# A two-layer hybrid flow trunk on one core: the edges of the expert stage, the squares of the norms and the last norm rearranged

## What is computed

```python
for l in range(DEPTH):                                  # DEPTH = 2
    sh1, sc1, gt1, sh2, sc2, gt2 = ada_mod(cond, w_ada[l], b_ada[l])   # silu(cond) @ w_ada + b_ada
    h = rms_norm(y, g_attn[l]) * (1 + sc1) + sh1
    ... # three head groups: neighbourhood attention, latent attention, windowed attention
    y = y + gt1 * (concat(o_na, o_mla, o_swa) @ w_out[l])
    h = rms_norm(y, g_ffn[l]) * (1 + sc2) + sh2
    y = y + gt2 * moe(h)        # 16 experts in 4 groups; best group, then the top 2 of it
y = rms_norm(y, g_final)
```

## Time and profile before

| what | value |
|---|---|
| median of 3 runs | 1250.95 us (1248.72 to 1256.21) |
| the profiled execution | 1255.41 us |
| its span in the profile | 1253.4 us |
| TensorE busy | 1152.9 us, 92% |
| VectorE busy | 772.4 us, 62% |
| ScalarE busy | 632.9 us, 50% |
| mean granted clock of TensorE | 0.947 of full |
| moved by the DMA queues | 314.35 MB |

### The profile page before, as it was taken

The page is one execution under the profiler, slowest core; times in us unless marked ns, Lnnn a source line. Parts: engine busy times, 40 slices in busy tenths (PEclk is TensorE's granted clock), DMA queues, the critical chain, the costliest instruction groups (busy, mean ns, idle before and its releaser), DMA issues.

```text
span 1253.4 us, 14864 instructions
## 1 busy us (share of the span) xinstructions
PE 1152.9 (92%) x5574; PEld 844.6 (67%) x5574; DVE 772.4 (62%) x1056; ACT 632.9 (50%) x751; POOL 127.8 (10%) x157
## 2 busy tenths in 40 slices
PE   6999998897899999999879998889789999999956
PEld 5576354554788888888666754455578888888846
DVE  1312356427698888888451233742768888988845
ACT  2201455315377777777320035631447777777721
POOL 2241100310100101010010011000000101010000
PEclk9899999999799999999969998999779999999985
DMA  9994478339489999999699140002549999999621
GB/s 330 335 309 169 145 264 280 100 109 377 148 321 372 359 376 366 383 375 367 221 345 240 68 168 16 1 1 81 245 158 352 369 375 378 377 364 369 257 87 75
DMA packets 81257, 314.35 MB, mean 251 GB/s; under 512 B 22766, under 2 KB 27100, under 8 KB 68396
## 3 DMA queue, kind: packets, MB, share of 16 engines
q1 hardware_dynamic: 65548, 279.17, 61.2%
q0 software_dynamic: 13152, 24.96, 6.0%
q10 hardware_dynamic: 2496, 9.44, 2.0%
HBM read 308.11 MB, written 26.38 MB: 267 GB/s over the span
## 4 chain that ended last, share of the span: by engine, by line
PE 84%; DVE 7%; issue 3%; ACT 3%; DMA 2%; SPq 0%; ACTq 0%; POOL 0%; POOLq 0%; DVEq 0%
PE bank L813 17%; PE bank L1072 14%; PE bank L1066 14%; PE bank L1067 14%; PE bank L795 3%; PE bank L941 3%; PE bank L820 3%; PE bank L740 2%; PE bank L1056 2%; PE bank L955 2%; ACT work L1295 2%; PE bank L733 2%; PE bank L973 1%; PE bank L1046 1%; PE bank L874 1%
## 5 line engine op out<-in xcount | busy, mean ns | idle before, releaser
L1791 DVE TENSOR_TENSOR ring_r<-ring,work_r 128x4096 fp32r<-128x4096 f32 x96 | 421.6, 4416 | 0.1
L1352 ACT ACTIVATE work_r<-ring 128x4096 fp32r<-128x4096 f32 x96 | 349.6, 3644 | 138.0 <-PE bank L1067 104.4
L1066 PE MATMUL bank<-work_r 128*128 128x512 f32 x768 | 310.1, 404 | 12.3 <-issue 5.1
L1067 PE MATMUL bank<-work_r 128*128 128x512 f32 x768 | 303.9, 396 | 0.0
L813 PE MATMUL bank<-hT,ring 128*128 128x384 f32 (+1 forms) x640 | 213.7, 493 | 3.3 <-ACT hT L1202 1.9
L1072 PE MATMUL bank<-ring_r,work_r 128*128 128x512 f32 x768 | 195.1, 396 | 0.4 <-DVE ring_r L1791 0.4
L813 PEld LDWEIGHTS bank<-hT,ring 128*128 128x128 f32 (+1 forms) x640 | 121.5, 192 | 88.0 <-issue 11.6
L1066 PEld LDWEIGHTS bank<-work_r 128*128 128x128 f32 x768 | 147.5, 192 | 43.9 <-issue 5.8
L1072 PEld LDWEIGHTS bank<-ring_r,work_r 128*128 128x128 f32 x768 | 144.2, 188 | 34.5 <-DVE ring_r L1791 0.8
L1067 PEld LDWEIGHTS bank<-work_r 128*128 128x128 f32 x768 | 147.1, 192 | 29.6
L1174 ACT ACTIVATE work<-bank 128x384 f32<-128x384 f32 (+6 forms) x79 | 38.0, 494 | 179.7 <-PE bank L813 89.3
(11 more groups left out here) (202 smaller groups left out, 1152.7 us busy)
## 6 DMA issues: line engine op xcount, KB each, us to landing
ring<-in_w_gate SPq DMA_DIRECT2D x32, 2048.0 KB, 11.5
ring<-in_w_up SPq DMA_DIRECT2D x32, 2048.0 KB, 12.3
ring<-in_w_down SPq DMA_DIRECT2D x32, 2048.0 KB, 12.3
ring<-in_w_ada SPq DMA_DIRECT2D x24, 2048.0 KB, 10.0
ring<-in_w_in SPq DMA_DIRECT2D x4, 2048.0 KB, 15.5
work<-yscr ACTq DMA_DIRECT2D x6, 1024.0 KB, 7.1
ring<-in_w_out SPq DMA_DIRECT2D x4, 1280.0 KB, 8.0
ring<-in_w_in SPq DMA_DIRECT2D x12, 256.0 KB, 6.9
```

The costliest lines, as they stand in the source:

```text
L1066: mm(b[:], x_hi[:, k, :], hi[:, k, half, :], start=(k == 0), stop=False)
L1067: last = mm(b[:], x_lo[:, k, :], hi[:, k, half, :], start=False, stop=False)
L1352: A_(w_hi[:, slot % 2, :], ring[slot][:], ACT.Copy).then_inc(s_hi, 1)
L1791: tt(ring_r[slot][:], ring[slot][:], w_hi[:, slot % 2, :].bitcast(F32), ALU.subtract).then_inc(s_lo, 1)
```

## The change

1. *Start.* g_final is no longer turned with the small vectors, the constant `rot` goes, and three more constants are cast to bf16.
2. *Squares.* VectorE adds the four blocks of each half tile in one reduction (`add_piece`, fp32, reading with a step of 384 words) into `sqr`; TensorE sums one product for each half tile instead of four. This holds at the start and behind layer 0.
3. *Expert 0's gate weights* are split by ScalarE and VectorE behind op5 of the output projection (`EARLY = 5`) instead of at the entry.
4. *Slots in bf16.* Mask, ranks, one-hots and the values of a token are bf16 (token number and tile offset apart, gate weight in three parts). All four groups of one-hots lie in hT. The first group's products come directly behind the rank and counts; the late modulation jobs, the other groups and the gate weights (48 products of three columns) come later, between expert 0's gate and up products. Expert 1's tokens have tiles of their own, and expert 0's activations are turned between gate and up of expert 1. Indices are made by a reduction of two values and one addition.
5. *Last norm on rows.* zT is turned back unscaled; ScalarE squares the rows in PSUM with a running sum (`fsum`), VectorE makes the root and scales the rows by it and by g_final, which a broadcast load has put on all partitions (`gfin`). The six outputs go by tiles.

The core of the diff:

```diff
+LAST_ROWS = [(DEPTH - 1, f"y{t}{h}") for t in range(2) for h in range(2)] + ["fo00", "fo01", (DEPTH - 1, "y20"), (DEPTH - 1, "y21"),
+                                                                             "fo10", "fo11", None, None, "fo20", "fo21"]
...
-        bS = (bA, bG, bU, bY[0])
+        bS = (bY[1], bY[0], bA, bY[1])
...
             def piece_sums(l, t, h):
 
-                pe.wait_ge(s_sq, squares_before(l, 0) + 2 * t + h + 1)
-                for k in range(4 * h, 4 * h + 4):
-                    last = mm(bN[:, t:t + 1], hT[:, k, t * P:(t + 1) * P], ones[:, 0:1], start=(k == 0), stop=(k == KT - 1))
+                pe.wait_ge(s_sqr, PIECES * l + 2 * t + h + 1)
+                last = mm(bN[:, t:t + 1], sqr[:, 2 * t + h, :], ones[:, 0:1], start=(h == 0), stop=(h == 1))
...
+                    by_slot(0)
+                    if p == 0:
+                        jobs_done()
...
                     tokens(0, 0, g0 + 16)
-                    pe.wait_ge(s_slot, NG * n + 3)
-                    gate_up(0, (0, 1))
-                    tokens(1, 1, g1 + 16)
-
-                    pe.wait_ge(s_slot, NG * (n + 1))
-                    turn_a(0)
+
+                    def second_tokens_and_slots():
+                        tokens(1, 1, g1 + 16)
+                        for q in range(1, NG):
+                            by_slot(q)
+                        weights_by_slot()
+
+                    gate_up(0, (0, 1), second_tokens_and_slots)
...
+                    if n == EARLY:
+                        act.wait_ge(*moe_land(l, 0, 0, 0))
+                        A_(w_hi[:, 0, :], ring[0][:], ACT.Copy).then_inc(s_hi, 1)
...
+            def add_piece(l, i):
+
+                t, h = divmod(i, 2)
+                v.wait_ge(s_sq, squares_before(l, 0) + i + 1)
+                nc.vector.tensor_reduce(sqr[:, i, :], hT[:, 4 * h:4 * h + 4, t * P:(t + 1) * P].rearrange("p k n -> p n k"),
+                                        AX.X, ALU.add).then_inc(s_sqr, 1)
...
-            piece_squares(lambda t, h: (DEPTH - 1, f"y{t}{h}"))
             for t in range(NT):
-                copy(f"fo{t}0", xrows[:, t, 0:512], 512)
+                for h in range(2):
+                    b = take(act, f"fo{t}{h}")
+                    A_(hT[:, 4 * h:4 * h + 4, t * P:(t + 1) * P], b[:].rearrange("p (k s) -> p k s", k=4), ACT.Square,
+                       accum_out=fsum[:, t, h:h + 1]).then_inc(s_fsq, 1)
```

More of the change, by code:

```diff
@@ L242, in sb, with both @@
             return ctx.enter_context(nc.sbuf_tensor(name, shape, dt))
-        def both(name, shape):
+        def both(name, shape, halves=False):
             with ExitStack() as first:
                 plain = first.enter_context(nc.sbuf_tensor(name, shape, F32))
-            return plain, sb(name + "_r", shape, F32R)
+            if not halves:
+                return plain, sb(name + "_r", shape, F32R)
+            with ExitStack() as first:
+                rounded = first.enter_context(nc.sbuf_tensor(name + "_r", shape, F32R))
+            return plain, rounded, sb(name + "_h", shape[:-1] + [2 * shape[-1]], BF16)
         def sem(name):
@@ L1029, in _, with jobs_done @@
                 for t in range(NT):
-                    last = mm(banks[7][:, 0:NE], ones, m[:, t, :], start=(t == 0), stop=(t == NT - 1))
+                    last = mm(banks[7][:, 0:NE], onesb[:], m[:, t, :], start=(t == 0), stop=(t == NT - 1))
                 last.then_inc(s_counted, 1)
-                for j in route[5:]:
-                    ada(j)
-                for bk in range(NB):
-                    pe.wait_ge(s_evac[bk], sum(JOB[j][0] == bk for j in LIST[:LIST.index((l, "y00") if l else (1, BETWEEN[0]))]))
+                def jobs_done():
+                    for j in route[5:]:
+                        ada(j)
+                    for bk in range(NB):
+                        pe.wait_ge(s_evac[bk], sum(JOB[j][0] == bk for j in LIST[:LIST.index((l, "y00") if l else (1, BETWEEN[0]))]))
@@ L1047, in experts, with weights_by_slot @@
                                           start=(t == 0 and e == 0), stop=(t == NT - 1), skip_group_check=True)
                         last.then_inc(s_slotp, 1)
+                    def weights_by_slot():
+                        pe.wait_ge(s_wts, l + 1)
+                        pe.wait_ge(s_cnt, l + 1)
+                        for t in range(NT):
+                            for e in range(NE):
+                                last = mm(banks[7][:, 3 * e:3 * e + 3], onehot[:, e // EPG, t, e % EPG, :], vals[:, t, e, 4:7],
+                                          start=(t == 0 and e == 0), stop=(t == NT - 1), skip_group_check=True)
+                        last.then_inc(s_slotw, 1)
@@ L1139, in _, with returned @@
                 pe.wait_ge(s_ys, done * NE)
-                for t in range(NT):
+                def returned(t):
                     pe.wait_ge(s_ysum, l * NT + t + 1)
@@ L1487, in rsqrt @@
                         chain(ins)
-                ins.then_inc(s_root, 1)
+                return ins
             def ada(l, j):
@@ L1878, in _ @@
                         evac((l, f"y{t}{h}"), ins)
+                        if 2 * t + h and l + 1 < DEPTH:
+                            add_piece(l + 1, 2 * t + h - 1)
+                if l + 1 < DEPTH:
+                    add_piece(l + 1, PIECES - 1)
                 read_out(v, (l, "y21"))
-            rsqrt((DEPTH, 0), D)
-            normalise_last("nfb")
+            v.wait_ge(s_fsq, 2 * NT)
+            chain(nc.vector.tensor_reduce(ns[:, 4, :], fsum, AX.X, ALU.add))
+            chain(ts(ns[:, 0, :], ns[:, 4, :], 1.0 / D, EPS, ALU.mult, ALU.add))
+            chain(newton())
+            v.wait_ge(s_gfin, 16)
             for t in range(NT):
-                b = take(v, f"fo{t}1")
-                evac(f"fo{t}1", tc(xrows[:, t, 512:1024], b[:]))
+                for h in range(2):
+                    half = slice(512 * h, 512 * h + 512)
+                    evac(f"fo{t}{h}", stt(xrows[:, t, half], bank(f"fo{t}{h}")[:], ns[:, 1, t:t + 1], gfin[:, half], ALU.mult, ALU.mult))
         @block.gpsimd
```

266 lines of the change are left out of this document (159 added, 107 removed).

## The result

The changed kernel took 1241.54 us (median of 8 runs, 1238.36 to 1245.94) against 1251.43 us (8 runs, 1248.72 to 1256.21): ratio 0.9914, 95% interval 0.9893 to 0.9935. Two later sets, each beside new runs of the kernel before, gave 1237.87 us (4 runs, ratio 0.9887, 0.986 to 0.9914) and one run of 1234.77. I had forecast 1252, within 1239 to 1260, and "no change". By the first set it is 9.9 us, 0.9%, faster, a little under the 1% that I had called distinguishable from no change, and by the second 13.6 us, 1.1%. The intervals of both exclude no change.

The account below looks back on a forecast made before the run. TensorE was taken to bound the kernel (84% of the chain), with only start, entries, seam and tail able to move. Terms summed to +1.2 us: profiled 1255.41 becomes 1256.6, scaled to the median 1252, range 1239 to 1260.

Parts of the forecast that it names:

- "no change": Whole kernel: a measured time within about 1% (12.5 us) of the kernel before, chance 0.80.
- Start, +1.6: Program start: TensorE idles some 3 us before the fourth modulation chunk's products, which then run at half clock; +1.6 us.
- Entries, -1.5 and -4.1: Up to each layer's first gate product: it comes 1.5 us earlier in layer 0, 4.1 us earlier in layer 1.
- Gate to down, +7.35 and +6.8: First gate to first down product: added small products, half clock and a weight-subtraction stall; +7.35 us layer 0, +6.8 layer 1.
- a rival (1245, chance 0.15): Cheap bf16 products: at 0.03 us each the 84 take 2.5 us instead of 5.9, twice -3.4; 1245 us, chance 0.15.
- Seam, -0.3: Behind layer 0: VectorE's strided reductions, 1.0 us each, replace most TensorE sums of squares; root 0.3 us earlier.
- Tail, -8.6: Last norm to the end: rows scaled after transposing back, so sums, spread and hT pass go; -8.6 us, within 0.7.
- my signs of being wrong: A gate product waits for its gather, the steady loops change, or the small products hold the clock.
- the rivals: Clock holds 1244 (0.17); cheap products 1245 (0.15); slower 1267.6 (0.06); double-rate one-hots 1248 (0.05); all removed work gained 1237 to 1239 (0.12).

Follow-up runs that it names:

- the run with the old sums: Changed kernel with the first norms' sums of squares (start and behind layer 0) made again as 24 TensorE products each, no VectorE reductions: 1240.67 us, ratio 0.9908.
- the tail alone: Kernel before with only the last norm changed to rows (transposes of zT, ScalarE's squares with accumulator, scaling of rows): 1243.52 us, ratio 0.993.
- the exchange on VectorE: Changed kernel with the subtraction of expert 1's up weights put ahead of that of expert 0's turned activations on VectorE: 1231.42 us, ratio 0.9833.

## Why the prediction was wrong

Point by point, by its own steps (forecast, then the difference of medians):

- **Start, +1.6: +1.1.** Right, by the same two rows (wait for the fourth chunk, 3.43 us at half clock). But the run with the old sums lost as much, so the new sums are not what caused it. All ten profiles with the rest of the change waited 2.6 to 4.3 us for the fourth chunk and ran its products at half clock, or for the most part; the three of before and that of the tail alone waited 1.3 us or less and kept the clock. Which part of the change makes that difference stays open.
- **Entries, -1.5 and -4.1: -2.1 and -5.2.** The mechanism was right: one subtraction in front of the gate product instead of two serial steps, 6.0 and 3.9 us when it is put back. The 0.4 us by which I let the squares slip did not exist (47.07 and 47.08 us): from the spread to the first product of the mask it was 0.3 us more than before, where I had 0.9. One-hots cost 3.69 us for six, as I took them. The Trainium skill (Vector Engine (DVE) Microarchitecture Reference, section 5.1: no double rate where one element is read many times in a two-source operation on 2-byte operands) is borne out by that row. The gather was a near miss: TensorE waited for it (5.79 us), and VectorE for its copy 0.24 us, so two chains end together here. The bf16 slots were not undone by themselves, so their share of the entries is argued and not shown.
- **Gate to down, +7.35 and +6.8: +3.9 and +2.4. This is the step that failed.** I priced the small bf16 products at 0.07 us by the share that their weight load has of the fp32 one, 5.9 us for 84. They took 0.025 to 0.026, 2.1 to 2.5 us in all, just under the lower bound of 0.03 that I had carried. That is 3.4 to 3.8 us a layer, and with it the sign. I had this price before me as a rival (1245, chance 0.15), and its mechanism came true. I had also let the clock fall behind them every time, where it fell in one of the three profiles. The Trainium skill's rule on weight-path perf modes (TensorE: Matmul & The Clock Gate: weights of any type but fp32 load several chunks at once) pointed there; for bf16 these rows bear it out, for fp32r the 0.216 us of the earlier trace rows at half clock still speak against it. The 32 cycles that I took from that section of the Trainium skill stand there as theory for fp8, so they were never a price for these products. The rest of this term was sized well: the stall on expert 1's up weights 2.07 us (forecast 1.9), the up product 7.2 us where the clock fell (7.7). The base of the term was read 0.24 us too long in each layer: 354.13 and 946.02 are steps of the chain, while TensorE's first down product starts at 353.89 and 945.78, so the 29.65 and 30.2 us before were 29.41 and 29.97, and 37.0 us now would have been +7.6 and +7.0.
- **Seam, -0.3: -0.7**, and about -2 against the one profile with the old sums. Reductions with a step of 384 words took 1.02 us each, as taken; where the rest comes from was not settled.
- **Tail, -8.6: -10.6.** ScalarE's last square ended 13.6 us behind the first addition, where I had 15.6. Some 1.5 us of this are the clock in the last sixteen transposes (2.33 us; at half clock, with eight in 1.97, I estimate 3.8); the rest lies in front of them.
- **Not in my sum:** the loop's period, +0.06 us an expert and +1.8 in all (that the loops change was among my signs of being wrong); the falls of the clock in the first attention, which made the profile that I worked from 3.6 us longer than others. I had scaled its 1255.41 to the median of 1251 by a factor, where part of the distance was this one event.

The range's lower end, 1239.0, lies under the measured 1241.5, by the width that I had left for the rivals and not by the sum. What was wrong is the sign: a sum of +1.2 where the edges give -9.4. Of these 10.6 us, the small products are about 7.2 by their price and 0.6 by the rest of that term, the tail 2.0, the entries 1.7, start and seam 0.9, and the loop takes back 1.8.

Read by edits: the tail alone brings 8 to 10.6 us and the early split 7 to 10, while the stretch from gate to down takes back 6.3 and the loops 1.8. Of these 6.3 us, 4.5 are the wait that the exchange on VectorE removes.

## What to carry to other kernels

A product that the trace does not show should be priced from its own operand type: between 0.03 and 0.216 us I scaled by the weight load alone (98 against 190 ns), and that ratio is not the product's price, which was 0.025. After such a move look at what now stands in each engine's queue between two waits: exchanging two subtractions on VectorE gave at least 4.5 us, a third to a half of what the whole change brought. And before working from one profile of a kernel whose runs spread by 0.6%, compare edges that no edit touches with a second one.

## What I had not expected of the hardware

- The clock falls or stays after the same 1.9 us of idling in the same program, at 43 us and again at 155 us: both in three profiles (195.65 us), in part in one (192.7), neither in ten (192.0). What decides was not found.
- A busy TensorE does not always hold its clock with small bf16 products: 0.91 over the 4.29 us of 168 of them, then 0.50; with 84 it fell in 4 layers of 18.
- The loop over the experts, with the same products in the same order, runs at 18.00 instead of 17.94 us a period in every profile of every kernel that has the changed expert code, and at 17.94 in the four profiles without it, at a granted clock of 1.00 in both. The output projection, on the contrary, takes 47.07 us in both. The cause was not looked for by a run and stays open.
